# Stick-breaking attention: ScalarE works block by block from one table set, instead of in groups of three blocks

## The reference

```python
for blk in range(t_len // SB_BLOCK):              # blocks of 128 queries, all earlier keys
    z = einsum('bhtd,bhsd->bhts', qb, kb) * scale
    causal = s_idx < t_idx
    log_beta = log_sigmoid(z)
    log_one_minus = where(causal, log_sigmoid(-z), 0.0)
    tail = lax.cumsum(log_one_minus, axis=3, reverse=True) - log_one_minus
    weights = masked_exp(causal, log_beta + tail)
    outs.append(einsum('bhts,bhsd->bhtd', weights, vb))
y_a = merge_heads(a_out) * silu(a_g)
```

## Time and profile before

| What | Value |
|---|---|
| Median of three runs | 5353.64 us |
| The profiled execution: time, and span | 5354.07 us, 5351.9 us |
| PE busy, DVE busy, ACT busy in the span | 4827.9 us (90%), 2726.8 us (51%), 1057.5 us (20%) |
| The stage: first quarter, first score, last op, next stage's first matmul | 2076.3, 2093.7, about 2495.2, 2499.5 us |
| Instructions | 43527 |

### The profile page before, as it was taken

How to read it: one execution, slowest core, us unless ns; L and a number is a source line. 1 busy time by engine, 2 the same in 40 slices (tenths; PEclk the granted TensorE clock), 3 DMA queues, 4 the chain that set the end, 5 groups by cost and what they waited for, 6 DMA issues and landing times. The chain is left out here.

```text
span 5351.9 us, 43527 instructions
## 1 busy us (share of the span) xinstructions
PE 4827.9 (90%) x16184; PEld 2473.9 (46%) x16184; DVE 2726.8 (51%) x3797; ACT 1057.5 (20%) x1562; POOL 379.3 (7%) x251
## 2 busy tenths in 40 slices
PE   8988788899999798888987989988999988999996
PEld 3434443344444344333653334436888843444442
DVE  6546554745555532223534564544344355666767
ACT  1003321200000001333322021232433421110101
POOL 0015311000000000001211000000000010000000
PEclk9999899999999899988998999997999989999998
DMA  2221202111111122111123022443112021111112
GB/s 100 81 94 44 83 32 110 63 47 39 48 46 64 68 79 79 40 41 68 55 95 112 32 106 87 158 159 93 43 36 51 18 110 64 40 47 40 44 43 79
DMA packets 191862, 366.20 MB, mean 68 GB/s; under 512 B 102975, under 2 KB 104527, under 8 KB 190888
## 3 DMA queue, kind: packets, MB, share of 16 engines
q1 hardware_dynamic: 175720, 319.92, 17.7%
q0 software_dynamic: 7872, 28.84, 1.5%
q10 hardware_dynamic: 8064, 14.68, 0.7%
HBM read 264.65 MB, written 98.73 MB: 68 GB/s over the span
## 5 line engine op out<-in xcount | busy, mean ns | idle before, releaser
L172 PE MATMUL mlp_bank<-mlp_u,mlp_s 128*128 128x512 f32 x864 | 381.9, 598 | 5.4 <-DVEq L256 5.4
L172 PE MATMUL p_bank<-p_t,p_s 128*128 128x512 f32 x720 | 319.3, 600 | 11.7 <-DVEq L885 11.7
L172 PE MATMUL mlp_bank<-mlp_x,mlp_s 128*128 128x512 f32 x608 | 273.3, 592 | 0.0
L172 PEld LDWEIGHTS mlp_bank<-mlp_u,mlp_s 128*128 128x128 f32 x864 | 166.1, 193 | 216.8 <-issue 213.3
L236 ACT ACTIVATE mlp_p<-mlp_bank 128x512 f32<-128x512 f32 x70 | 41.4, 591 | 953.9 <-PE mlp_bank L172 929.8
L172 PEld LDWEIGHTS p_bank<-p_t,p_s 128*128 128x128 f32 x720 | 138.0, 192 | 188.7 <-issue 187.1
L246 DVE TENSOR_TENSOR mlp_sum_u<-mlp_bank,mlp_p 128x512 f32<-128x512 f32 x70 | 48.4, 692 | 308.1 <-PE mlp_bank L172 306.9
L172 PEld LDWEIGHTS mlp_bank<-mlp_x,mlp_s 128*128 128x128 f32 x608 | 115.5, 190 | 145.4 <-issue 140.4
L172 PE MATMUL mlp_bank<-tail_z,mlp_s 128*128 128x512 f32 x352 | 158.2, 592 | 0.0
L236 ACT ACTIVATE p_p<-p_bank 128x512 f32<-128x512 f32 x30 | 17.9, 597 | 677.8 <-PE p_bank L172 677.8
L628 ACT ACTIVATE mlp_cv<-mlp_raw,mlp_taps 128x1024 f32<-128x1024 f32 x44 | 54.6, 1240 | 455.4 <-DVEq L643 455.4
(11 more groups left out here) (742 smaller groups left out, 9339.0 us busy)
## 6 DMA issues: line engine op xcount, KB each, us to landing
mlp_w<-in_w_up SPq DMA_DIRECT2D x38, 512.0 KB
proj<-p_ev SPq DMA_DIRECT2D x38, 512.0 KB, 3.6
p_w<-in_w_in SPq DMA_DIRECT2D x28, 512.0 KB, 5.8
first_w<-in_w_in SPq DMA_DIRECT2D x24, 512.0 KB, 4.1
hgnx_merge_g<-proj SPq DMA_DIRECT2D x8, 1536.0 KB, 7.2
tail_mlp_w<-in_w_up SPq DMA_DIRECT2D x22, 512.0 KB
p_w<-in_w_out SPq DMA_DIRECT2D x16, 512.0 KB, 4.4
mid_mlp_w<-in_w_up SPq DMA_DIRECT2D x16, 512.0 KB
```

The source lines that it names most:

```text
L172: mm = nc.tensor.matmul(self.bank[product - 1][:, :], lhs[:, p, :], rhs(name, p), start=p == 0, stop=p == kp - 1)
```

## The change

Four things move. ACT goes block by block: `decay(n)`, `weight(n-3)`, `logarithm(n)`. The Sigmoid of a head's gate leaves the head's start: the first is issued before the first `keep`, the others after block 6 of the head before; behind each of them one table set is named that is to serve Exp and Ln. On DVE `logw(n-1)` follows `sum_up(n)` in every block, the last one follows the loop, and `take` goes behind `logw`. On PE the wait for `padded` moves behind the first four quarters.

```diff
@@ block.tensor
-                pe.wait_ge(padded, 1)
                 def gate_quarter(m):
...
                 for m in range(STICK_AHEAD):
                     gate_quarter(m)
+                pe.wait_ge(padded, 1)
@@ block.scalar
+                def gate_sigmoid(h):
+                    act.wait_ge(loaded[h % 2], (h // 2 + 1) * 48)
+                    nc.scalar.activation(SG[h % 2][:, :], G[h % 2][:, :], ACT.Sigmoid).then_inc(sig_ready, 1)
+                    nc.scalar.preload_act_table_set("natural_log_exp_and_others")
...
                         h = i * 2 + s
+                        if h == 0:
+                            gate_sigmoid(0)
                         if s == 0:
                             keep(i, 0)
-                        act.wait_ge(loaded[s], (i + 1) * 48)
-                        nc.scalar.activation(SG[s][:, :], G[s][:, :], ACT.Sigmoid).then_inc(sig_ready, 1)
-                        for g in range(0, NB + 3, 3):
-                            for n in range(g, min(g + 3, NB)):
+                        for n in range(NB + 3):
+                            if n < NB:
                                 decay(h, n)
-                            for n in range(max(g - 3, 0), g):
-                                weight(h, n)
-                            for n in range(g, min(g + 3, NB)):
+                            if n >= 3:
+                                weight(h, n - 3)
+                            if n < NB:
                                 logarithm(h, n)
-                            if g == 0 and s == 0:
+                            if n == 2 and s == 0:
                                 keep(i, 1)
+                            if n == 6 and h + 1 < H:
+                                gate_sigmoid(h + 1)
@@ block.vector
                             soft(h, n)
+                            sum_up(h, n)
+                            if n:
+                                logw(h, n - 1)
                             if n % 2 == 0 and 0 < n <= 4 * STICK_SHARE:
                                 take(STICK_AHEAD // 2 + 2 * STICK_SHARE * h + n // 2 - 1)
-                            sum_up(h, n)
-                            if n % 3:
-                                logw(h, n - 1)
-                            if n % 3 == 2:
-                                logw(h, n)
                             if n == 7:
                                 finish(h, s, 0)
+                        logw(h, NB - 1)
```

## The result

The changed kernel takes 5265.59 us in the median of four runs (5262.31 to 5268.87); the kernel before, run beside it, 5354.53 us (5345.07 to 5356.88). The ratio is 0.9837, with a 95% interval of 0.982 to 0.9854: faster by 1.6%, 89 us. The forecast was 5276 us with a range from 5263 to 5292. The profiled execution has a span of 5263.9 us, 88.0 less than before.

What follows compares the result with a forecast made beforehand. PE was taken to bound the heads, with up to 83.5 us of waits and slow clock to lose; less 6.8 for clock falls, plus 1.1 for the memsets, 77.8 us faster: 5276 us, range 5263 to 5292.

Steps and rivals of the forecast that it cites:

- Bound and waits: Four heads: PE sets the pace and waits 49.1 us for results of `soft`, at the starts of ACT's groups of three.
- A head at full clock: PE without waits or slow clock: heads sum to 317.3 us against 400.8, so up to 83.5 us can go.
- Table loads: ACT in this stage: 40 loads of 1.283 us become eight; only what stands in PE's waits is worth anything.
- Head start: First `stick_lb` ready 2.45 us after the first score, needed at 3.42: the wait goes, cover 1.0 us.
- Order in the loop: ACT and DVE queues in the new block order: a full iteration of cover everywhere, so no PE wait.
- last head: Iterations 9 to 11 without a quarter: PE 2.8 us, DVE and ACT some 2.4; tight, nothing counted, 1.5 us if slower.
- The clock: Thin scores at each head's start: one clock fall a head, 4 x 1.7 = 6.8 us taken off the gain, bounds 0 and 12.
- rival 1: Full clock throughout the heads, no falls: 84.6 us faster, 5269 us; chance 0.16.
- The memsets: Stage's start: PE no longer held by the memsets until 2076.30 and could start 1.1 us earlier.
- Rival 2: Named table not kept, two loads a block: waits at head starts and in the last head, 5294 us; chance 0.11.
- Rival 3: Each block waits because Ln(n) needs values from iteration n-1: 224 us slower, 5578 us; chance 0.04.
- Rival 4: No change: the gain is lost to the next stage, waiting for its first weights; chance 0.02.

Runs made afterwards that it cites:

- ln_first: table_only with the three Ln ahead of the three weights in each group of three on ACT; 5286.92 us, heads 336.1.
- small_gap: Changed kernel with two Copy operations (1.06 and 0.29 us) on ACT between the first block's Exp and Ln in each head; 5270.62 us, heads 325.7.
- pad_only: Kernel before with only PE's wait for the memsets moved behind the first four quarters; 5350.34 us, ratio 1.0.
- no_named_table: Changed kernel without the line that names one table set for Exp and Ln; 5273.96 us, heads 324.6.
- larger_gap: small_gap with the second Copy as long as the first (2.1 us in all); 5273.2 us, heads 328.2.
- table_only: Kernel before with Sigmoids moved off the heads' starts and one named table for Exp and Ln, groups of three kept; 5321.75 us, heads 362.3.
- merged: Changed kernel with a diagonal block's score as one matmul, its tail's later-keys part likewise; 5260.38 and 5263.43 us, heads 308.3.

## Why the prediction was right, and where it was off

**Bound and waits.** PE bound, its waits due to `soft` at ACT's groups: right. The four waits a head shrank or went in three steps, each with what the step took away (38.5, 26.2 and 21.1 us of heads), and the queue reading of the earlier trace rows, a Ln behind a `weight` that waits for PE, has its own run in ln_first.

**A head at full clock.** Forecast 82.4, 82.4, 82.4 and 68.3 us plus 1.8; measured, from first score to first score with the transposes counted in, 82.2, 82.4, 82.2 and 68.2. "Up to 83.5 us can go" came out as 85.8. In the second head, which came to 81.8 without its transposes, scores 0 to 2 take 3.26 us and not 3.42, iteration 0 5.42 and not 5.53, iteration 8 6.98 and not 7.1.

**Table loads.** Eight left of 40, as said. **Head start:** 2.45 us forecast, 2.42 measured; cover 0.84 instead of 1.0. Its account of before holds for two heads only: in the second and the last the Sigmoid was done before the first score arrived. **Order in the loop, last head, moved Sigmoids:** no wait of PE anywhere, as said, for POOL or SP neither. In the last head iteration 8 has no quarter either, which the prediction's "iterations 9 to 11" leaves out; nothing hung on it.

**The clock.** This is the term that failed: "I count one fall a head", 4 x 1.7 = 6.8 us, with bounds of 0 and 12. It measured zero, all four windows at 1.00. The reading of the earlier trace rows was at fault. I took it that scores alone had pulled the clock down, since it fell 0.25 us after the last one. But in those 0.25 us PE was idle, and small_gap shows that with 0.34 us of idle time in such scores the clock falls in three heads of four, while with the same scores without it (both profiles of the changed kernel, eight heads) it never did. Why a head with the pause is sometimes spared stays open. So the case that came true is rival 1, full clock throughout, priced at 5269 us with a chance of 0.16; the measured 5265.6 is 3.4 us below it, of which 2.3 are the heads' sum and the rest is within the run-to-run spread. The result lies within the stated range, but below the 5268 to 5285 us that the forecast's own case was given; the range held it because it made room for rival 1. The gap rule of the Trainium skill ("TensorE: Matmul & The Clock Gate", section "Why this matters for your kernels"), which I had weighed against that row, agrees with the changed kernel's trace: no idle time in the heads, granted clock 1.00. Its long gaps are not the whole story: in thin work 0.34 us was enough in five heads of seven.

**The memsets.** 1.1 us forecast. From memset to first score before took 18.47 us, the changed kernel 18.04 and pad_only, which has this edit alone, 17.10: 0.4 and 1.4 us less. The mean of the ten profiles without the wait is 1.5 us below that of the three with it. PE starts 1.35 us earlier in both kernels; how much of that reaches the first score goes with the clock's rise, and no total shows it.

**Rival 2** was priced 11.6 + 6.6 us over the forecast and did not come; its mechanism, run by itself as no_named_table, cost 9.6 us of heads. **Rival 3**, a wait in every block, did not come, as the distance of n-6 says. **Rival 4** neither: the next stage's first matmul follows the heads' end by the same 5.0 us as before.

## What to carry to other kernels

When a fast engine works for a full one, look at what is queued ahead of the result that is wanted next. Here a Ln stood behind an Exp that waited for the full engine itself, and moving it ahead was worth two thirds of what the named table and the moved Sigmoids gave together. Batching by table set is a means to save loads, not an end: with a set that holds both functions the batches have no reason left here, and even with 101 loads the order by blocks beat batches with 40. Price a wait of TensorE with the clock behind it: of 85.8 us, 49.1 were waits and about 36 slow clock.

## What the runs showed of the hardware that I had not expected

- A head's start, scores of 64 rows and 128 to 384 columns with their masks and one tail of 128 columns back to back, 5.15 us of them to the first quarter, kept the granted clock at 1.00. With an idle time of 0.34 us among them it fell to 0.50 in five heads of seven (small_gap and no_named_table), with 1.1 us in four of four (larger_gap). With a delay of 0.14 to 0.18 us, of which the profile shows 0.02 us or nothing as idle, it fell in none of three.
- Elsewhere longer pauses left it at 1.00: 0.78 to 0.79 us between full quarters, waiting for `stick_ev`, in all thirteen profiles, and 2.04 us before score 9 of table_only's second head, though other waits of 2.0 us in that kernel were followed by a fall. The length of a pause alone does not decide; what else does was not shown.
- A fall behind a pause of 0.34 us cost 1.7 us in three heads and 3.3 in two: five to ten times the pause.
- The heads took 315.0 us in both profiles of the changed kernel, while the spans were 5263.9 and 5258.5 us. The other pairs agree as well: 308.3 and 308.3 us for merged, 400.8 and 400.8 for before and pad_only, whose heads have the same code. A difference of a few us in one stage can be read from its own stretch when the total can't show it.
